# Lower halves ahead of gathers, last dots moved into the softmax stage, and weight tiles loaded in pairs

## What is computed

```python
def _peer(h, wq, subkeys, u_tab, v_tab):
    xt = h.reshape(T, D)                                   # T = 512, D = 1024
    q = (xt @ wq).reshape(T, 8, 2, 128)
    s = jnp.einsum('thpd,hpnd->thpn', q, subkeys)
    sv, si = lax.top_k(s, 16)
    comb = (sv[:, :, 0, :, None] + sv[:, :, 1, None, :]).reshape(T, 8, 256)
    cs, ci = lax.top_k(comb, 16)
    ia = jnp.take_along_axis(si[:, :, 0], ci // 16, axis=-1)
    ib = jnp.take_along_axis(si[:, :, 1], ci % 16, axis=-1)
    idx = ia * 128 + ib
    g = jax.nn.softmax(cs, axis=-1)
    ...
        a = jnp.einsum('td,thkd->thk', xb, u_tab[eb])      # eb = idx, gb = g, by blocks of tokens
        w = gb * jax.nn.gelu(a, approximate=False)
        return jnp.einsum('thk,thkd->td', w, v_tab[eb])
...
ffn = _peer(h, peer_wq, peer_subkeys, peer_u, peer_v)
gate = jax.nn.sigmoid(h @ ple_gate_w + ple_gate_b)
h = _layer_norm(ALPHA * h + ffn + gate * (p @ ple_w), ln2_g, ln2_b)
```

## Time and profile before

| | before |
|---|---|
| median of 3 runs | 1327.51 us (1326.87 to 1327.83) |
| profiled execution | 1327.52 us, span 1325.7 us |
| PE busy | 1281.0 us, 97% |
| DVE busy | 1135.9 us, 86% |
| ACT busy | 688.1 us, 52% |
| POOL busy | 699.8 us, 53% |
| moved by DMA | 404.90 MB, 305 GB/s over the span |

### The profile page before, as it was taken

The page is one execution under the profiler, slowest core; times in us unless marked ns, Lnnn a source line. Parts: engine busy times, 40 slices in busy tenths (PEclk is TensorE's granted clock), DMA queues, the critical chain, the costliest instruction groups (busy, mean ns, idle before and its releaser), DMA issues.

```text
span 1325.7 us, 22565 instructions
## 1 busy us (share of the span) xinstructions
PE 1281.0 (97%) x7713; PEld 715.1 (54%) x7713; DVE 1135.9 (86%) x2410; ACT 688.1 (52%) x962; POOL 699.8 (53%) x411
## 2 busy tenths in 40 slices
PE   6999999999989999999979999999999999999997
PEld 3554555556656677777745555555344444444444
DVE  8866488889997899889758988989899898898997
ACT  5652655556666788888824343433333334333342
POOL 4741333457775566766624666657574464455502
PEclk9999999999999999999999999999999999999999
DMA  7222422268888799999999999999999999999952
GB/s 300 96 103 72 128 96 80 80 217 282 308 325 296 244 364 390 404 396 396 394 410 335 355 383 365 363 363 405 395 380 402 402 402 390 395 403 400 395 197 106
DMA packets 130342, 404.90 MB, mean 305 GB/s; under 512 B 12513, under 2 KB 48481, under 8 KB 128097
## 3 DMA queue, kind: packets, MB, share of 16 engines
q1 hardware_dynamic: 88800, 253.08, 51.8%
q0 software_dynamic: 41472, 151.01, 29.5%
HBM read 358.96 MB, written 44.56 MB: 304 GB/s over the span
## 4 chain that ended last, share of the span: by engine, by line
PE 61%; DMA 17%; DVE 9%; issue 5%; ACT 3%; POOL 3%; SPq 1%; DVEq 0%; POOLq 0%; ACTq 0%; another core or an unknown queue 0%
DMA area<-gelu_scratch 14%; PE bank L785 14%; PE bank L773 12%; PE bank L774 12%; PE bank L775 12%; DVE cut L1472 4%; DMA raw<-tiles_dram 2%; DVE ple_gate L1949 2%; PE bank L1050 2%; POOL cut L637 2%; PE bank L800 2%; PE bank L994 1%; PE bank L992 1%; DVE area L1942 1%; PE bank L941 1%
## 5 line engine op out<-in xcount | busy, mean ns | idle before, releaser
L785 PE MATMUL bank<-cut,area 128*128 128x512 f16 x2208 | 483.7, 380 | 3.4 <-DVE cut L1472 3.4
L773 PE MATMUL bank<-hT,cut 128*128 128x352 f16 (+1 forms) x1216 | 393.8, 324 | 17.8 <-POOL cut L637 8.9
L775 PE MATMUL bank<-hT,cut 128*128 128x352 f16 (+1 forms) x1216 | 393.5, 324 | 0.2 <-issue 0.2
L774 PE MATMUL bank<-hT,cut 128*128 128x352 f16 (+1 forms) x1216 | 393.6, 324 | 0.0
L785 PEld LDWEIGHTS bank<-cut,area 128*128 128x128 f16 x2208 | 216.2, 98 | 261.9 <-DVE cut L1472 5.3
L1472 DVE SCALAR_TENSOR_TENSOR cut<-raw,cut 128x1024 f16<-128x1024 f32 x214 | 270.0, 1263 | 80.0 <-ACT cut L1081 55.7
L1081 ACT ACTIVATE cut<-raw 128x1024 f16<-128x1024 f32 x214 | 222.5, 1052 | 222.3 <-DMA raw<-tiles_dram 199.1
L637 POOL TENSOR_TENSOR cut<-raw,cut 128x1024 f16<-128x1024 f32 x80 | 170.5, 2142 | 173.4 <-DVE window_word L1717 93.6
L773 PEld LDWEIGHTS bank<-hT,cut 128*128 128x128 f16 x1216 | 119.2, 98 | 95.9 <-issue 11.9
L775 PEld LDWEIGHTS bank<-hT,cut 128*128 128x128 f16 x1216 | 119.2, 98 | 75.7
L774 PEld LDWEIGHTS bank<-hT,cut 128*128 128x128 f16 x1216 | 119.2, 98 | 74.2 <-issue 0.2
(11 more groups left out here) (226 smaller groups left out, 1600.1 us busy)
## 6 DMA issues: line engine op xcount, KB each, us to landing
raw<-tiles_dram SPq DMA_DIRECT2D x298, 512.0 KB
gates_scratch<-area SPq DMA_DIRECT2D x12, 2048.0 KB, 13.2
area<-gates_scratch SPq DMA_DIRECT2D x31, 768.0 KB
gelu_scratch<-gelu_out SPq DMA_DIRECT2D x88, 192.0 KB
area<-gelu_scratch SPq DMA_DIRECT2D x22, 768.0 KB
norm_rows<-norms_dram SPq DMA_DIRECT2D x3, 1024.0 KB, 7.6
hn<-x_dram SPq DMA_DIRECT2D x4, 512.0 KB, 5.3
out_dram<-hn SPq DMA_DIRECT2D x3, 512.0 KB, 2.6
```

The costliest lines, as they stand in the source:

```text
L773: nc.tensor.matmul(dst, w[0], hT[:, 0, k, 0:width], start=(k == 0), stop=False)
L774: nc.tensor.matmul(dst, w[0], hT[:, 1, k, 0:width], start=False, stop=False)
L775: last = nc.tensor.matmul(dst, w[1], hT[:, 0, k, 0:width], start=False, stop=(k == KD - 1))
L785: mm = nc.tensor.matmul(bank[:, 2 * tt + h, :], lhs(a)[:, tt * P:(tt + 1) * P], cut[:, t.slot, b, h * HALF:(h + 1) * HALF], start=(first a ...
```

## The change

- Selection: four lower halves move from POOL to DVE, one in the lookup of each of the units 5 to 8 (`plain_lo`); in the last windows POOL makes all of its lower halves before it gathers. The first eight gathers wait for window 11 now, not for 10's end.
- The shift of the gates stands before window 18, and ACT's exponent ahead of the softmax tiles.
- Dots: four are made in the softmax stage (`SOFT_DOTS`), six fewer in the KEPT stage; the eights hold 24, 23, 23. POOL issues eight gathers instead of four between the three hn adds and the first lower half of the gate stage.
- Tiles from 88 on are laid out and loaded in pairs of 1 MB, 8 KB for each partition, into six slots, `raw` having grown by two; one of these held `gate_b`. A pair of tiles n and n+1 waits for the lower half of tile n-5.
- The last store of gates stands behind one more load, and the first weight waits for that store. Loops of SP and ACT are unrolled.

```diff
-LOWS_IN_WINDOW = (4, 2, 3, 1, 3, 1, 3, 2, 2, 0, 3, 2, 5, 4, 5, 4, 3, 3, 6)
+LOWS_IN_WINDOW = (4, 2, 3, 1, 3, 1, 3, 2, 2, 0, 3, 2, 5, 4, 5, 4, 4, 2, 2)
+SOFT_DOTS = 4
+LOOKUP_LOWS = (5, 6, 7, 8)
...
+T_PAIRS = T_U + U_TOPK + U_SOFTMAX + LOAD_AHEAD
+PAIR_RING = 3
...
-KEPT_DOTS = 12
-EIGHT_DOTS = (23, 23, 22)
+KEPT_DOTS = 6
+EIGHT_DOTS = (24, 23, 23)
...
-        raw = sb("raw", [P, RING, D])
+        raw = sb("raw", [P, 2 * PAIR_RING, D])
-        gate_b_row = sb("gate_b_row", [P, D])
+        gate_b_row = raw[:, 2 * PAIR_RING - 1, :]
...
+            def load_pair(t):
+                if t.pair >= PAIR_RING:
+                    sp.wait_ge(lo_cut, t.n - 2 * PAIR_RING + 2)
+                elif 2 * t.pair < RING:
+                    sp.wait_ge(lo_cut, T_PAIRS - RING + 2 * t.pair + 2)
+                else:
+                    sp.wait_ge(gate_biased, TT)
+                src = tiles[t.n:t.n + 2].rearrange("a p n -> (a p n)").rearrange("(p x) -> p x", p=P)
+                sp.dma_start(raw[:, t.raw_slot:t.raw_slot + 2, :].rearrange("p a n -> p (a n)"),
+                             src).then_inc(pair_in[t.pair % PAIR_RING], 16)
...
                     load_gates(0, 0)
                     load_gates(0, 1)
+                if c == U_EARLY - U_KEPT + 2:
                     store_gates(GCH - 1, 1, TD // 4)
...
+                if (n - 2) // 2 in LOOKUP_LOWS and n % 2 == 0:
+                    low += 1
+                    pool.wait_ge(lo_cut, low)
-                for j in range(count):
+                for _ in range(count):
                     pool_low(Tile(low))
                     low += 1
-                    if n > 2 * LATTER_HALF and j:
-                        for _ in range(begun, min(begun + 2, EARLY, dotted + EARLY_SLOTS)):
-                            gather(begun)
-                            begun += 1
-                if n == 2 * LATTER_HALF:
+                if n == 2 * LATTER_HALF + 1:
                     pool.wait_ge(ids_done, 1)
-                if n >= 2 * LATTER_HALF:
+                if n > 2 * LATTER_HALF:
                     for _ in range(begun, min(EARLY, dotted + EARLY_SLOTS)):
...
-            for n in range(EARLY, EARLY + ROW_RING):
+            for n in range(EARLY, EARLY + ROW_RING + SOFT_DOTS):
                 if n == EARLY + FREE_SLOTS:
                     pool.wait_ge(ple_added, ND)
                     pool.wait_ge(gated, TT)
...
+            act.wait_ge(gate_shift, 1)
+            nc.scalar.activation(picked[:, 2], picked[:, 2], ACT.Exp).then_inc(gate_exp, 1)
             for j in range(U_SOFTMAX):
...
+            def plain_lo(t):
+                dve.wait_ge(hi_cut, t.n + 1)
+                dve.wait_ge(tile_used, t.n - RING + 1)
+                dve.wait_ge(lo_cut, t.n)
+                nc.vector.tensor_tensor(cut[:, t.slot, 1, :], raw[:, t.raw_slot, :], cut[:, t.slot, 0, :],
+                                        ALU.subtract).then_inc(lo_cut, 1)
...
+                if unit in LOOKUP_LOWS:
+                    plain_lo(Tile(lookup_low(unit)))
                 for width in (K * K // 2, K * K // 4, K * K // 8):
...
+                if unit == len(SELECTION) - 1:
+                    shift_gates()
                 open_window(2 * unit + 2)
...
                 if tt == 2:
+                    for n in range(SOFT_DOTS // 2):
+                        dot(EARLY + n)
                     split_lo(softmax_tiles[4])
                     split_lo(softmax_tiles[5])
...
             split_lo(softmax_tiles[6])
+            for n in range(SOFT_DOTS // 2, SOFT_DOTS):
+                dot(EARLY + n)
             dve.wait_ge(gated, TT)
...
                 if i == 0:
                     dve.wait_ge(gates_copied, 1)
+                    dve.wait_ge(gates_stored[1], 16 * (GCH // 2))
...
-        "tiles": c(tiles),
+        "tiles": c(np.concatenate([tiles[:T_PAIRS], tiles[T_PAIRS:].reshape(-1, 2, P, D).transpose(0, 2, 1, 3).reshape(
+            -1, P, D)])),
```

More of the change, by code:

```diff
@@ L95 @@
 T_END = T_ALL - RING
+T_PAIRS = T_U + U_TOPK + U_SOFTMAX + LOAD_AHEAD
+PAIR_RING = 3
+assert T_PAIRS % RING == 0 and (T_ALL - T_PAIRS) % 2 == 0
 STORED = (N_LATE - U_KEPT) // 4
@@ L110 @@
 EARLY = sum(map(sum, DOTS_IN_UNIT))
-KEPT_DOTS = 12
-EIGHT_DOTS = (23, 23, 22)
+KEPT_DOTS = 6
+EIGHT_DOTS = (24, 23, 23)
 EIGHT_SUMS = (24,)
 LATE_SUMS = (10, 10, 10, 10, 10, 9, 9, 9, 9, 9, 9)
-assert U_GATES + EARLY - EXTRA + KEPT_DOTS + sum(EIGHT_DOTS) == HK and sum(EIGHT_SUMS) + sum(LATE_SUMS) == HK
+assert SOFT_DOTS + U_GATES + EARLY - EXTRA + KEPT_DOTS + sum(EIGHT_DOTS) == HK and sum(EIGHT_SUMS) + sum(LATE_SUMS) == HK
 assert len(EIGHT_DOTS) + len(EIGHT_SUMS) == EIGHTS and len(LATE_SUMS) + 1 == N_LATE // 8 and N_LATE % 8 == 0
@@ L177, in __init__, with raw_slot, pair @@
         self.round = c // RING + (k // RING) * it if k else c // RING
+    @property
+    def raw_slot(self):
+        if not isinstance(self.n, int) or self.n < T_PAIRS:
+            return self.slot
+        return (self.n - T_PAIRS) % (2 * PAIR_RING)
+    @property
+    def pair(self):
+        return (self.n - T_PAIRS) // 2
     def plus(self, d):
@@ L383, in layer @@
         tile_in = [sem(f"tile_in{s}") for s in range(RING)]
+        pair_in = [sem(f"pair_in{s}") for s in range(PAIR_RING)]
         hi_cut, lo_cut, tile_used = sem("hi_cut"), sem("lo_cut"), sem("tile_used")
@@ L518, in build_gates @@
                             store_gates(2 * it - 1, 1, 16 * it)
-            build_gates(0)
-            with sp.Fori(1, U_GATES // 8) as it:
+            for it in range(U_GATES // 8):
                 build_gates(it)
@@ L680, in _ @@
                 pool_low(t)
-                for n in range(EARLY + ROW_RING + 2 * pair, EARLY + ROW_RING + 2 * pair + 2):
+                for n in range(EARLY + ROW_RING + SOFT_DOTS + 2 * pair, EARLY + ROW_RING + SOFT_DOTS + 2 * pair + 2):
                     gather(n)
-            for n in range(EARLY + ROW_RING + U_GATES, EXTRA + 2 * HK):
+            for n in range(EARLY + ROW_RING + SOFT_DOTS + U_GATES, EXTRA + 2 * HK):
                 gather(n)
@@ L1077, in _, with arrived @@
         def _(act):
+            def arrived(t):
+                if isinstance(t.n, int) and t.n >= T_PAIRS:
+                    act.wait_ge(pair_in[t.pair % PAIR_RING], 16 * (t.pair // PAIR_RING + 1))
+                else:
+                    act.wait_ge(tile_in[t.slot], 16 * (t.round + 1))
             def split_hi(t):
-                act.wait_ge(tile_in[t.slot], 16 * (t.round + 1))
+                arrived(t)
                 free_slot(act, t)
-                nc.scalar.activation(halves_of(t)[:, 0, :], raw[:, t.slot, :], ACT.Copy,
+                nc.scalar.activation(halves_of(t)[:, 0, :], raw[:, t.raw_slot, :], ACT.Copy,
                                      scale=t.scale).then_inc(hi_cut, 1)
             def scale_and_split_hi(t, later=None):
-                act.wait_ge(tile_in[t.slot], 16 * (t.round + 1))
-                nc.scalar.activation(raw[:, t.slot, :], raw[:, t.slot, :], ACT.Copy,
+                arrived(t)
+                nc.scalar.activation(raw[:, t.raw_slot, :], raw[:, t.raw_slot, :], ACT.Copy,
                                      scale=S_W).then_inc(raw_scaled, 1)
@@ L1425, in _ @@
             both(0)
-            with act.Fori(1, len(EIGHT_DOTS)) as e:
+            for e in range(1, len(EIGHT_DOTS)):
                 both(e)
@@ L1454, in final_normal @@
                                      scale=rstd[:, t:t + 1]).then_inc(centred, 1)
-            with act.Fori(0, N_LATE // 8 - 1) as e:
+            for e in range(N_LATE // 8 - 1):
                 late(e)
@@ L1717, in open_window, with shift_gates, lookup_low @@
                 nc.vector.memset(window_word[:], 0.0).then_inc(window_open, 1)
+            e_view = picked[:, 2].rearrange("p t (h k) -> p (t h) k", k=K)
+            def shift_gates():
+                own.link(nc.vector.tensor_copy(e_sum, e_view[:, :, 0]))
+                nc.vector.tensor_tensor(e_view, e_view, e_sum.unsqueeze(2).to_broadcast([P, TT * HEADS, K]),
+                                        ALU.subtract).then_inc(gate_shift, 1)
+            def lookup_low(unit):
+                return POOL_FIRST + sum(LOWS_IN_WINDOW[:2 * unit + 2]) + LOOKUP_LOWS.index(unit)
             def top_k(unit, first_head, heads, first_tile, tiles):
@@ L1896, in build_gates @@
                             onehots(4 * it + 2 * s + j // 2, j // 2)
-                        dot(EARLY + 8 * it + 4 * s + j)
+                        dot(EARLY + SOFT_DOTS + 8 * it + 4 * s + j)
                         if j % 2:
@@ L1909, in _ @@
                 for j in range(KEPT_DOTS * c // U_KEPT, KEPT_DOTS * (c + 1) // U_KEPT):
-                    dot(EARLY + U_GATES + j)
+                    dot(EARLY + SOFT_DOTS + U_GATES + j)
             dve.wait_ge(ones_done, 2)
@@ L1990, in both @@
                             step(j)
-            first = EARLY + U_GATES + KEPT_DOTS
+            first = EARLY + SOFT_DOTS + U_GATES + KEPT_DOTS
```

27 lines of the change are left out of this document (13 added, 14 removed).

## The result

The changed kernel takes **1315.12 us** (median of 4 runs, 1314.54 to 1315.61) against 1327.19 us (1326.76 to 1327.83) of the kernel before on the same chip: a ratio of 0.9909, 95% interval 0.9893 to 0.9925. The forecast was 1313.8, range 1304 to 1327. The profiled execution has a span of 1313.7 us.

A forecast was written before the change was run, and what follows sets the result against it. PE (TensorE) was taken as the bound, busy 1281.0 of 1325.7 us. From 1327.5, +0.6 (selection and hand-over), -10.9 (wait before 697) and -3.4 (wait before 956.7) gave 1313.8 us, range 1304 to 1327.

The forecast's parts named there:

- selection and hand-over: Selection to gate stage: tile 84 starts 1.2 us earlier, a low clock costs 1.8; sum +0.6 us, -4.0 to +8.9.
- wait before 697: PE's 8.85 us wait for tile 138 and 2.0 us of low clock go: -10.9 us, bounds -5.8 and -10.9.
- wait before 956.7: PE's 3.15 us wait for tile 206 and its low clock mostly go: -3.4 us, bounds -1 and -4.9.
- the signs that it named: Trace marks at PE's selection waits, one-hots, tile 84, 688 to 701, and ACT's wait for tile 206 (under 7 us).
- four old waits: Selection: PE's long waits for POOL's lower halves, the first 1.64 us, the last 2.00; forecast to go.
- the step on window 18: Selection: DVE ends between 2.5 us later and some us earlier, so no shift of window 18, 1.5 either way.
- The held gather: Hand-over: a gather at 446.78 took 2.27 us against 0.96, outlasting a DVE tensor_tensor, against the skill's rule.
- tile 138's part: Before 697: pair 138/139, now ahead of the store, lands by 677, where ACT wants it at 681.5.
- The argument on the second pair: Before 697: pair 140/141, behind the store and some 3 MB of gathers, lands at 686.5; ACT wants it at 688.7.
- A (hand-over early): Rival at the hand-over: adds end at 434.2, eight gathers run free, no low clock; 1309.2 us, chance 0.18.
- B (prefetch worth half): Rival on loads: pair 140/141 late (-5.8), the 956 stall gives 1, hand-over +2; 1322.7 us, chance 0.20.
- C: Rival from 889 to 1120: 8 KB tile packets delay row gathers, up to 1.3 us a pair; 1339.8 us, chance 0.12.

The follow-up runs named there:

- x_first8: Changed kernel with the selection's first eight gathers back at window 10's end, as before: 1312.39 us, ratio 0.9891 to the kernel before.
- x_sel: Changed kernel with the selection as before (no lower half on DVE, gathers between POOL's halves): 1322.69 us, ratio 0.9971 to the kernel before.
- x_hand: Changed kernel with four of the eight gathers moved behind the first halves of the gate stage: 1309.87 us, ratio 0.9872 to the kernel before.
- x_kept: Changed kernel with no dots in the softmax stage, twelve in the KEPT stage and 23, 23, 22 in the eights: 1306.51 us, ratio 0.9845.
- x_store: Changed kernel with the last gate store ahead of the pair 138/139 again: 1314.97 us, ratio 0.9905 to the kernel before.
- eight combinations: Kernels with the store's place, the pairs and fewer dots each changed or not; PE's wait near 690 runs from 8.85 us (kernel before) to 0 (changed).
- x_4k: Changed kernel with pairs laid out as before, two rows of 4 KB a partition instead of one of 8 KB: 1318.54 us, ratio 0.9939.
- x_single: Changed kernel with tiles loaded one by one into four slots, as before: 1322.6 us, ratio 0.9959 to the kernel before.
- x_both: Changed kernel with the edits of x_hand and x_first8 together: 1304.28 us, ratio 0.9825 to the kernel before.

## Why the prediction was right, and where it was not

**The total** came out 1.3 us above the forecast. That it is so close is partly luck: the hand-over was 4.1 us worse than forecast, and 2.1 us that the forecast did not count made up half of this. By the table of matmuls:

| term | forecast | measured |
|---|---|---|
| selection and hand-over | +0.6 (-4.0 to +8.9) | +4.7 |
| wait before 697 | -10.9 (-5.8 to -10.9) | -11.0 (from +4.7 to -6.3) |
| wait before 956.7 | -3.4 (-1 to -4.9) | -3.6 (from -6.3 to -9.8) |
| rest | 0 | -2.1 (before: waits of 0.26 at 1055.94, 1.57 at 1290.85) |

Of the signs that it named, two came: PE is full from 688 to 701 at 1.00, and ACT's wait for tile 206 is 6.38 us, under 7. PE does wait for a lower half between 300 and 400, 2.79 us at 309.19; it is at the first one-hots at 446.3 instead of 442, and at tile 84 at 456.7 instead of 452. The windows moved back by 2.1, 3.4 and 6.5 us (14, 16 and 18), which it had called a sign of being wrong, yet the four old waits did not return.

**Selection: the step on window 18 failed.** The four long waits and the short ones did go, as worked out. But the forecast took no shift of window 18, 1.5 either way, and it came 6.5 later. The causes can be read off the rows. POOL's last half of an odd window still waits for ACT, since ACT goes at PE's pace; it now runs into another instruction of the lookup, 3.03 us against 1.22, in each of the units 5 to 7, so the time that L1765 gave back was spent again. And the first eight gathers had been moved behind such a waiting half, which held DVE's dots by 4.1 us and made a new wait of PE, 2.79 us and then 1.2 GHz; x_first8 takes this away, the collisions in units 5 and 6 with it, and 4.2 of the 6.5 us. The other 2.3 come in the last unit: windows 16 to 18 take 27.1 us (27.2 in x_first8) against 24.1 before and 24.9 in x_sel. There DVE has one moved half more and the shift of the gates, and window 16's fourth half, which waits for ACT, runs beside

```profile
385.34 2.34 DVE L1798 TENSOR_TENSOR area<-area 128x64 f32<-128x64 f32 x2
```

where x_sel has 0.36 us for the same two. The prediction named the moved wait of window 10 nowhere: of the step that was moved it counted the gathers between the halves, not the first eight.

**Hand-over: the mechanism was right; its start was off.** PE, over 5 us ahead at 393, lost it all again to DVE and to POOL's eight gathers. From the first gather to tile 84 15.2 us were forecast and 15.1 measured; the gathers behind the one-hots took 0.94 each, as taken. DVE needed 36.6 us of work in the 38.8 from window 18 to the end of the adds, where 39.7 without idle time were forecast. The adds ended at 441.3 instead of 437 (bounds 434.2 to 440) because window 18 was late. The low clock cost 1.6 us behind tile 84, and 0.7 ahead of it that the wait for tile 84 covers, where 1.8 was charged. x_hand and x_kept show what this place is worth: 5 and 9 us.

The held gather was seen again: 2.28 us at 444.88, beside L1948 from 444.06, and 0.94 once the one-hots were over. The Trainium skill (SBUF — State Buffer, Who interferes with whom) infers that a tensor_tensor does not hold up the writing of descriptors; this trace differs as the one before did.

**The wait before 697: right size, wrong cause.** The forecast gave tile 138's part to the place of its pair ahead of the store. x_store shows that the place is worth nothing once the other two edits are in, and the eight combinations show that no single edit is the cause. The argument on the second pair, which added up all bytes in SP's queue and the gathers, with six dots instead of twelve, is the one that fits the eight combinations. The first weight, forecast for 694.5, came at 699.06, as much earlier as PE, and cost nothing.

**The wait before 956.7: about right.** Of the two parts the rows of 8 KB were taken too small: 0 to 0.9 us over 31 us was the bound, 2.6 of the 4.6 us behind 948 is what the traces of x_4k and x_single show, 1.6 of it later than 960. The forecast looked at one wait and missed that the same margin is used up again in later eights, and at the end.

**Rivals.** A (hand-over early) and B (prefetch worth half) did not come about in the changed kernel. x_both reaches A's times (tile 84 at 447.92), but with the adds at 437.5, not 434.2, and with four gathers behind them. C did not come about: PE is busy 160.00 of 160.00 us from 960 to 1120 with 8 KB rows, and the DMA moved more, not less. Its price was too low as well: from 889 to 1120 SP loads 29 pairs, not 20, so 1.3 us each would have been 38. Whether the engines take turns by packet, as the Trainium skill has it (DMA: Bandwidth & Descriptors, Queues, rings and completion order), no run here settles.

## What to carry to other kernels

Removing a wait on an engine that runs ahead brings only the distance to the next stage that is late for another reason: ask at once which engine hands over there, and what was put in front of that hand-over (here four gathers, 5 us). When a helper's work is moved ahead of other work in its queue, look whether that work itself waits, since then all behind it waits too. A stall with several transfers in front of it can be a matter of the sum of their bytes, and edits that seem to be its cure can each be replaced by another; take them away one at a time and together before one is named.
